# Expert rows gathered by quarters and turned on VectorE instead of TensorE, in a one-core mixture-of-experts layer

## The chip, the cores and the metric

One NeuronCore of a Trainium2 chip runs the whole layer as one program. The metric is the device time of one execution in microseconds (us). All data are float32.

## The reference

The layer takes a residual stream x of 1024 tokens by 1024 features. It runs three gated token mixers side by side (attention, a matrix memory, a gated recurrence), merges them, and adds the result to x. Then a fine-grained mixture of experts follows, which is the part that the change touches:

```python
scores = sigmoid(h @ router_w)              # 1024 tokens, 64 experts
idx, wts = top 8 experts of each token      # 8192 assignments
for each block of rows of one expert e:     # rows sorted by expert
    xb  = h[rt]                             # gather the rows of its tokens
    hid = silu(xb @ w1[e]) * (xb @ w3[e])   # 1024 -> 256
    y.at[rt].add((hid @ w2[e]) * rw)        # 256 -> 1024, scatter-add
y = y + (silu(h @ ws1) * (h @ ws3)) @ ws2   # the shared expert
```

## The kernel before

Up to about 1600 us it computes the mixers, their merge, the router (`route`, `choose`, `slots`) and the shared expert. Each token's normalised row goes to `h2_d` in DRAM, and (token, weight) pairs are scattered into per-expert lists in `list_d`, 8 lists of 128 slots for each expert, of which every partition holds one slot of every list.

Then comes the expert stage, which loops over a table of work items. An item is one expert with at most 256 tokens: a first tile of 128 rows and, if it has more, a second one. A tile with at most 64 rows runs as a half tile, on shorter matmuls. This run has 67 items with 93 tiles. For item i:

- SyncE loads the expert's weights, 2 MB for the first product (`load_up`, L483 and L484, four buffers) and 1 MB for the second (`load_down`, L488, two buffers), each as soon as an item ahead has freed its buffer.
- GpSimd gathers the item's rows from `h2_d` three items ahead (`gather`, L712, one indirect DMA for a tile, one row of 4 KB for each partition), once the list indices are there (`e_idx`) and once the rows that lay in the buffer have been turned (`e_Tb`). After that it issues the scatter-add of item i-1 (`scatter`, L716), when the scatter before has landed and VectorE has weighed the output.
- TensorE (`pe_item`) runs the first product of item i (`up`, L1285; `up_half`, L1289), then turns the rows of item i+1 so that the features lie on the partitions (`turn_rows`, L1253, eight 128x128 transposes for a tile, into PSUM), then the second product of item i-1 (`down`, L1342; `down_half`, L1348), with the transposes of the hidden rows of item i (L1387, L1391) between its two halves.
- ScalarE copies the turned rows from PSUM to `xgT` (`rows_turned`, L1732, two copies for a tile), applies silu (L1736) and copies the turned hidden rows (L1739).
- VectorE multiplies the hidden rows (L2402), takes the indices of item i+3 (L2425), weighs the output of item i-1 (L2377, L2381, L2383) and takes its lists (L2418 to L2420).

The order on each engine is that of the program; engines wait for each other through semaphores. The feature order in `h2_d` is chosen in L2205 so that partition p of a turned row block holds rows 8p to 8p+7 of the weights.

Of the kernel before, what the change touches and what calls it, by code (L numbers as in the profile page):

```python
# [15 lines left out]

# [10 lines left out]
P = 128  # L27
# [8 lines left out]
def layer_kernel(nc, a, out):  # L36
# [24 lines left out]
    with ctx:  # L61
# [140 lines left out]
        lists2 = view(4096, NE * NT, 2)  # L202
        xg = [[view(12288, D), view(13312, D)], [view(20480, D), view(9248, D)]]
        xgT = view(14336, KD, 2 * P)
# [4 lines left out]
        idx = sb("idx", [P, 4, 2], I32)  # L209
# [15 lines left out]
        NDMA = {"sh0": 2}  # L225
# [22 lines left out]
        def bank_free(u):  # L248

            if U_B + 2 <= u < U_C:  # L250
# [57 lines left out]
        s_dst, s_ls = sem("s_dst"), sem("s_ls")  # L308
# [5 lines left out]
        e_Ta, e_Tb, e_xTa, e_xTb, e_H, e_si, e_hid, e_hT, e_hc, e_O, e_ob = (  # L314
            two(n) for n in ("Ta", "Tb", "xTa", "xTb", "H", "si", "hid", "hT", "hc", "O", "ob"))
        e_w += [sem(f"e_w{b}") for b in (2, 3)]
        e_v += [sem(f"e_v{b}") for b in (2, 3)]
        e_red, e_idx, e_idx1, e_sc = (sem("e_" + n) for n in ("red", "idx", "idx1", "sc"))
        to_clear = [*e_xg[0], *e_xg[1], *e_Ta, *e_Tb, *e_xTa, *e_xTb, *e_H, *e_si, *e_hid, *e_hT, *e_hc, *e_O, *e_ob,
                    e_red, e_idx, e_idx1, e_sc, *e_w[2:], *e_v[2:]]  # L320
# [89 lines left out]
        def _(sp):  # L410
# [14 lines left out]
            def load_block(n):  # L425
# [9 lines left out]
                elif kind == "wb":  # L435
                    src = a["w_branch"][0, j].rearrange("(k p) n -> p k n", p=P)
                    dst = flat(dst).rearrange("p (k n) -> p k n", k=4)
                elif kind == "wo":
                    src = a["w_out"][0][:, BW * j:BW * (j + 1)].rearrange("(k p) n -> p k n", p=P)
                else:  # L440
                    sp.dma_start(dst[:, :, 0:FF], a["sh_w1"][0].rearrange("(p k) f -> p k f", k=KD)).then_inc(s_ring[n % 3], 16)
                    src, dst = a["sh_w3"][0].rearrange("(p k) f -> p k f", k=KD), dst[:, :, FF:2 * FF]
# [88 lines left out]
        def _(pool):  # L531
# [86 lines left out]
            for n, row in ((1, 48), (2, 40)):  # L618
                g.dma_start(mod_d[n].rearrange("(k j m) -> j k m", k=KD, j=8),
                            foxmask[row:row + 8, :].rearrange("j (k m) -> j k m", k=KD)).then_inc(s_rd, 16)  # L620
            pool.wait_ge(s_rd, 128)
# [34 lines left out]
            for n in range(48):  # L656
# [6 lines left out]
                if n == 4:  # L663
# [5 lines left out]
                    g.dma_start(rwt, a["router_w"][0].rearrange("(p k) e -> p k e", k=KD)).then_inc(s_rw, 16)  # L669
# [34 lines left out]
            pool.wait_ge(s_ls, 16 + 16 * NT * TOPK)  # L704
            rows = list_d.rearrange("(p r) c -> p r c", p=P)
# [13 lines left out]
            def fetch_first(n, q, p):  # L719
                with pool.If(n > HALF):  # L720
                    gather(xg[0][p], idx[:, q, 0:1], P).then_inc(e_xg[0][p], 16)
                with pool.Else():
                    gather(xg[0][p], idx[:, q, 0:1], HALF).then_inc(e_xg[0][p], 16)
                pool.nop()

            def fetch_second(n, q, p):
                with pool.If(n > P):
                    with pool.If(n > P + HALF):
                        gather(xg[1][p], idx[:, q, 1:2], P).then_inc(e_xg[1][p], 16)
                    with pool.Else():  # L730
                        gather(xg[1][p], idx[:, q, 1:2], HALF).then_inc(e_xg[1][p], 16)
# [15 lines left out]
            pool.wait_ge(e_Tb[0], 1)  # L747
# [6 lines left out]
            def fetch_ahead(it, q):  # L754
# [3 lines left out]
                with pool.If(n_3 > 0):  # L758
                    pool.wait_ge(e_Tb[0], now)
# [51 lines left out]
        def _(pe):  # L811
# [339 lines left out]
            def route(i):  # L1151
                pe.wait_ge(s_h2c, i + 1)
                if i == 0:
                    pe.wait_ge(s_rw, 64)
# [96 lines left out]
            def turn_rows(j, x):  # L1251
                for k in range(KD):
                    mm = t.transpose(psum[:, 2 * j + k // 4, (k % 4) * P:(k % 4 + 1) * P], x[:, k * P:(k + 1) * P], ident[:, :])  # L1253
                    if k == KD // 2 - 1:
                        mm.then_inc(e_Ta[j], 1)
                mm.then_inc(e_Tb[j], 1)

# [4 lines left out]
            for x in (*e_H, *e_hT, *e_O, e_Ta[1], e_Tb[1]):  # L1262
                pe.sem_inc(x, 1)
            turned, seconds, outs = Count(pe, "turned"), Count(pe, "seconds"), Count(pe, "outs")
            fetched = [Count(pe, f"fetched{p}", 0, 16) for p in range(2)]
# [3 lines left out]

            def turn_second(p):  # L1270
                fetched[p].up()
                outs.wait(e_ob[1])
                fetched[p].wait(e_xg[1][p])
                turn_rows(1, xg[1][p])
                turned.up()

            def turn_first(p, fetches):
                pe.wait_ge(e_xg[0][p], fetches)
                turn_rows(0, xg[0][p])
# [4 lines left out]
            def up(j, h, r, k):  # L1284
                return t.matmul(bank(4 + j), xgT[:, k, P * j:P * (j + 1)], up_piece(h, r, k), start=(k == 0), stop=(k == KD - 1))  # L1285

            def up_half(j, b, k):
                for f in range(FK):
                    mm = t.matmul(psum[HALF * f:HALF * (f + 1), 4 + j, :].rearrange("p (w n) -> p w n", w=2)[:, :, 0:P], xgT[:, k, P * j:P * j + HALF],  # L1289
                                  w13[b][:, :, k, f * P:(f + 1) * P], start=(k == 0), stop=(k == KD - 1))  # L1290
                return mm

            def up_half_first(b, now):
                for k in range(KD):
                    if k == KD // 2:
                        pe.wait_ge(e_xTb[0], now)
# [8 lines left out]
            def up_first(n, h, r, now):  # L1305

                with pe.If(n > HALF):
                    for k in range(KD):
                        if k == KD // 2:
                            pe.wait_ge(e_xTb[0], now)  # L1310
# [1186 lines left out]
```

## Time and profile before

| | before |
|---|---|
| median of 3 runs | 2582.93 us (2582.93 to 2586.4) |
| profiled execution, from its first to its last instruction | 2584.8 us |
| TensorE busy | 2512.4 us, 97% |
| VectorE, ScalarE, GpSimd busy | 1029.0, 579.2, 417.5 us |
| mean granted TensorE clock | 0.993 of full speed |
| DMA | 440.86 MB, mean 171 GB/s |

The profiled execution's own time is its span, 2584.8 us; no other time of it is given. The expert stage, as it is used below, goes from the first `up` at 1608.94 us to the last `down` at about 2562 us.

### The profile page before, as it was taken

The page shows a single profiled execution, that of the slowest core. Times are in us where ns is not written, and L with a number is a line of the kernel's source. Part 1 is how long each engine was busy: PE and PEld are TensorE (multiplying, and loading weights), DVE is VectorE, ACT ScalarE, POOL GpSimd, SP SyncE. Part 2 cuts the span into 40 slices and gives each one's busy share as a digit, 9 for nine tenths or more (in the row PEclk, how much of TensorE's full clock was granted, in tenths as well). Part 3 has the DMA queues.
Part 4 walks back from the last instruction along what each step waited for, and adds up shares of the span by engine and source line. Part 5 has one row for each costly group of instructions (what it writes and reads, how often), then busy time and mean ns, then how long its engine had stood idle before and what let it go on. Part 6 is the DMA issues. An engine that isn't in the chain of part 4 may idle for free.

```text
span 2584.8 us, 35212 instructions
## 1 busy us (share of the span) xinstructions
PE 2512.4 (97%) x9350; PEld 1271.5 (49%) x9351; DVE 1029.0 (40%) x2548; ACT 579.2 (22%) x1078; POOL 417.5 (16%) x418
## 2 busy tenths in 40 slices
PE   6999999999999999999999999999999999999996
PEld 3444555555455556555444554445444444444443
DVE  3365443444465545554245756121222122222221
ACT  3311333332311331331111121111111111211110
POOL 0000000000210000000111435122222222222221
PEclk9999999999999999999999999999999999999998
DMA  9122243432723232222333116787889889989994
GB/s 269 52 49 75 77 116 96 107 109 73 200 54 82 82 94 80 76 96 95 124 108 133 58 41 235 260 263 230 256 277 360 289 284 344 349 269 330 344 295 92
DMA packets 128164, 440.86 MB, mean 171 GB/s; under 512 B 18220, under 2 KB 20404, under 8 KB 110928
## 3 DMA queue, kind: packets, MB, share of 16 engines
q1 hardware_dynamic: 86560, 306.91, 34.3%
q0 software_dynamic: 41520, 132.86, 19.7%
q8 instruction: 50, 0.82, 0.1%
q14 instruction: 34, 0.28, 0.0%
HBM read 369.85 MB, written 77.20 MB: 173 GB/s over the span
## 4 chain that ended last, share of the span: by engine, by line
PE 93%; DMA 4%; issue 1%; DVE 0%; ACT 0%; POOLq 0%; SPq 0%; POOL 0%; DVEq 0%
PE psum L862 34%; PE psum L1285 16%; PE psum L1342 8%; PE psum L1120 6%; PE psum L1137 4%; PE psum L1289 3%; PE psum L1253 3%; PE psum L1181 2%; PE psum L1077 2%; PE psum L1348 2%; DMA out_x<-mem,put 2%; PE psum L956 2%; PE psum L946 2%; PE psum L965 1%; DMA mem<-in_exp_w 1%; PE psum L1204 1%
## 5 line engine op out<-in xcount | busy, mean ns | idle before, releaser
L862 PE MATMUL psum<-mem 128*128 128x512 f32 x2048 | 910.1, 594 | 2.0 <-ACT mem L1485 2.0
L862 PEld LDWEIGHTS psum<-mem 128*128 128x128 f32 x2048 | 377.4, 191 | 416.9 <-issue 415.9
L1285 PE MATMUL psum<-mem 128*128 x1008 | 445.2, 597 | 6.6 <-issue 5.5
L1285 PEld LDWEIGHTS psum<-mem 128*128 128x128 f32 x1008 | 191.3, 191 | 253.9 <-issue 253.7
L1342 PE MATMUL psum<-mem 128*128 128x512 f32 x504 | 234.8, 598 | 2.0 <-DMA mem<-in_exp_w 1.0
L2402 DVE TENSOR_TENSOR mem<-mem,psum 128x256 f32<-128x256 f32 x93 | 39.2, 421 | 433.4 <-ACT mem L1736 428.1
L716 POOL DMA_INDIRECT out_x<-mem,put x93 | 142.6, 1534 | 345.8 <-issue 233.2
L1532 ACT ACTIVATE mem<-psum 128x512 f32<-128x512 f32 x128 | 75.8, 595 | 494.7 <-PE psum L862 491.9
L1736 ACT ACTIVATE mem<-psum 128x256 f32<-128x256 f32 x93 | 35.7, 384 | 615.6 <-PE psum L1285 491.6
L1120 PE MATMUL psum<-mem 128*128 128x512 f32 x384 | 165.0, 592 | 0.0
L712 POOL DMA_INDIRECT mem<-h_d,idx x93 | 95.4, 1026 | 390.0 <-DVE idx L2425 144.1
L2377 DVE SCALAR_TENSOR_TENSOR mem<-psum,lst,mem 128x1024 f32<-128x1024 f32 x63 | 80.9, 1284 | 171.7 <-PE psum L1342 161.3
L1342 PEld LDWEIGHTS psum<-mem 128*128 128x128 f32 x504 | 87.8, 190 | 91.4 <-issue 91.3
L1120 PEld LDWEIGHTS psum<-mem 128*128 128x128 f32 x384 | 72.9, 190 | 91.4 <-issue 91.4
L1137 PE MATMUL psum<-mem 128*128 128x512 f32 x256 | 112.3, 593 | 0.0
L1289 PE MATMUL psum<-mem 128*64 128x256 f32 x960 | 110.2, 382 | 0.7 <-issue 0.7
L1732 ACT ACTIVATE mem<-psum 128x512 f32<-128x512 f32 x186 | 98.5, 599 | 16.9 <-PE psum L1253 14.5
L1253 PEld LDWEIGHTS psum<-ident,mem 128*128 128x128 f32 x744 | 84.4, 142 | 35.5 <-issue 34.9
L1253 PE MATMUL psum<-ident,mem 128*128 128x128 f32 x744 | 95.3, 278 | 3.8 <-DMA mem<-h_d,idx 3.0
L1289 PEld LDWEIGHTS psum<-mem 128*64 128x64 f32 x960 | 66.6, 137 | 53.8 <-issue 23.8
L1967 DVE CUSTOM_DVE_ANT_0 mem<-psum,mem 128x512 f32<-128x512 f32 (+3 forms) x96 | 52.3, 557 | 99.8 <-PE psum L946 98.1
L683 POOL DMA_INDIRECT list_d<-mem x64 | 74.4, 1163 | 61.8 <-DVE mem L2259 44.7
(378 smaller groups left out, 2370.4 us busy)
## 6 DMA issues: line engine op xcount, KB each, us to landing
mem<-in_exp_w SPq DMA_DIRECT2D x201, 1024.0 KB
mem<-in_w_in SPq DMA_DIRECT2D x16, 2048.0 KB, 13.9
proj_d<-mem SPq DMA_DIRECT2D x104, 256.0 KB, 2.0
mem<-in_ada_w POOLq DMA_DIRECT2D x16, 1024.0 KB, 6.0
mem<-proj_d POOLq DMA_DIRECT2D x56, 256.0 KB, 2.9
mem<-proj_d POOLq DMA_DIRECT2D x20, 512.0 KB, 4.8
mem<-in_ada_w SPq DMA_DIRECT2D x4, 2048.0 KB, 19.8
mem<-in_w_branch SPq DMA_DIRECT2D x3, 2048.0 KB, 8.0
```

Source lines behind the costliest of these rows:

```text
L712: return g.indirect_dma_start(x[0:n], None, h2_d, bass.IndirectOffsetOnAxis(ap=i[0:n], axis=0), bounds_check=T - 1, oob_is_err=False)
L716: return g.indirect_dma_start(y_out, bass.IndirectOffsetOnAxis(ap=i[0:n], axis=0), x[0:n], None, bounds_check=T - 1, oob_is_err=True, comp ...
L862: mm = t.matmul(bank(unit_bank(u)), l, r, start=(k == 0), stop=(k == KD - 1))
L1120: mm = t.matmul(bank(n % 3), w[:, k, j * P:(j + 1) * P], yT[br][:, k, half * BW:(half + 1) * BW], start=(k == 0), stop=(k == 3))
L1137: mm = t.matmul(bank(half + 2 * (i == 1)), hT[:, k, i * P:(i + 1) * P], slot(("wo", half))[:, k, :], start=(k == 0), stop=(k == KD - 1))
L1253: mm = t.transpose(psum[:, 2 * j + k // 4, (k % 4) * P:(k % 4 + 1) * P], x[:, k * P:(k + 1) * P], ident[:, :])
L1285: return t.matmul(bank(4 + j), xgT[:, k, P * j:P * (j + 1)], up_piece(h, r, k), start=(k == 0), stop=(k == KD - 1))
L1289: mm = t.matmul(psum[HALF * f:HALF * (f + 1), 4 + j, :].rearrange("p (w n) -> p w n", w=2)[:, :, 0:P], xgT[:, k, P * j:P * j + HALF], w13[ ...
L1342: mm = t.matmul(bank(out_bank[j] + half), hidT[p][:, k, P * j:P * (j + 1)], w2[p][:, k, half * BW:(half + 1) * BW], start=(k == 0), stop=( ...
L1532: s.activation(dst, bank(unit_bank(u)), ACT.Copy).then_inc(s_ev, 1)
L1732: s.activation(xgT[:, 4 * half:4 * half + 4, P * j:P * (j + 1)], bank(2 * j + half).rearrange("p (k n) -> p k n", n=P), ACT.Copy).then_inc ...
L2377: v.scalar_tensor_tensor(out=ob[j][p], in0=banks(out_bank[j], 2), scalar=lst[:, q, j:j + 1], in1=g2b, op0=ALU.mult, op1=ALU.mult).then_inc ...
```

## The change

The gather of a tile becomes four indirect DMAs (two for a half tile). Each brings quarter rows of 1 KB for 32 tokens: partition 32i + b gets quarter i of token b of its group. VectorE then turns the tile with one transpose instruction that works on 32x32 blocks, straight from the gather buffer into `xgT`, of which there are now two. TensorE's `turn_rows` and ScalarE's `rows_turned` go, with their semaphores. The indices have to lie on the partitions in this new order, so the lists are loaded a second time in it (`first4`, `lists4`, four DMAs each) and the index of a quarter is 4 * token + quarter. The order of features in `h2_d`, and with it the loads of `router_w`, of the shared expert's weights and of two modulation rows, follow the quarters, in more and smaller DMAs. The hidden rows' transposes move from PSUM bank 5 to bank 1. `up_second` loses its waits for the copies.

```diff
-            def gather(x, i, n):
-                return g.indirect_dma_start(x[0:n], None, h2_d, bass.IndirectOffsetOnAxis(ap=i[0:n], axis=0),
-                                            bounds_check=T - 1, oob_is_err=False)
+            h2_q = h2_d.rearrange("t (i f) -> (t i) f", i=4)
+            def gather(x, j, q, groups, s):
+                for n in range(groups):
+                    g.indirect_dma_start(x[:, 2 * P * n:2 * P * (n + 1)], None, h2_q,
+                                         bass.IndirectOffsetOnAxis(ap=idx[:, q, j, n:n + 1], axis=0),
+                                         bounds_check=4 * T - 1, oob_is_err=False).then_inc(s, 16)
...
             pool.wait_ge(s_ls, 16 + 16 * NT * TOPK)
+            by_group = list_d.rearrange("(g b r) c -> b g r c", g=4, b=32)
+            for i in range(4):
+                g.dma_start(first4[32 * i:32 * i + 32], by_group[:, :, 0:3 * NT, :]).then_inc(s_l4, 16)
...
             fetch_second(tokens(pool, 1), 1, 1)
-            pool.wait_ge(e_Tb[0], 1)
+            for i in range(4):
+                g.dma_start(lists4[32 * i:32 * i + 32], by_group).then_inc(s_l4, 16)
+            pool.wait_ge(e_T, 1)
...
-                    pool.wait_ge(e_Tb[0], now)
+                    pool.wait_ge(e_T, now)
                     pool.wait_ge(e_idx, now)
...
                 with pe.If(n > 0):
-                    pe.wait_ge(e_xTa[0], now)
+                    pe.wait_ge(e_T, before)
...
                     pe.reg_mov(n_now, tokens(pe, i + 1))
-                    with pe.If(pe.snap(n_now) > P):
-                        turn_second(1 - r)
-                    pe.nop()
-                    with pe.If(pe.snap(n_now) > 0):
-                        turn_first(1 - r, 32 * it + 16 * h + 16 + 16 * r)
-                    pe.nop()
...
-            def rows_turned(j, half):
-                s.activation(xgT[:, 4 * half:4 * half + 4, P * j:P * (j + 1)], bank(2 * j + half).rearrange("p (k n) -> p k n", n=P),
-                             ACT.Copy).then_inc((e_xTa, e_xTb)[half][j], 1)
...
+            def turn_group(j, p, groups):
+                for _ in range(groups // 2):
+                    got[j][p].up()
+                got[j][p].wait(e_xg[j][p])
+                return v.transpose(xgT[p][:, :, P * j:P * j + 32 * groups].rearrange("p k (g b) -> p g k b", g=groups),
+                                   xg[j][p][:, 0:2 * P * groups].rearrange("p (g k a) -> p g k a", g=groups, k=KD))
...
             dve.wait_ge(s_ls, 16 + 16 * NT * TOPK + 32)
+            dve.wait_ge(s_l4, 128)
...
                         n = tokens(dve, i)
+                        with dve.If(tokens(dve, i + 1) > 0):
+                            turn_rows(tokens(dve, i + 1), (q + 1) % 2)
+                        dve.nop()
                         with dve.If(n > 0):
                             hidden_rows(n, dve.snap(i + 2))
```

`turn_rows` on VectorE calls `turn_group` for the second tile, if there is one, and then for the first, with 4 groups or 2, and raises `e_T`. For item 0 it is called before `shared_out(7)` and `put_lists`. In `residual` the one L2205 instruction becomes four, one for each quarter.

## Rows read from the trace of the kernel before

**Rows 1.** Windows of the expert stage: length, busy time of engines, clock, DMA share, GB/s.

```profile
1609.00:1650.00 41.00, 37.92 (x133) 19.07 (x134) 6.77 (x22) 7.09 (x16) 7.83 (x7) 0.92 0.74 255
1650.00:1900.00 250.00, 249.28 (x884) 123.01 (x883) 52.01 (x122) 41.23 (x94) 59.19 (x46) 1.00 0.82 255
1900.00:2150.00 250.00, 249.62 (x906) 122.11 (x907) 59.41 (x149) 41.55 (x94) 62.54 (x49) 1.00 0.92 305
2150.00:2220.00 70.00, 65.63 (x291) 31.91 (x288) 18.50 (x53) 13.52 (x30) 19.61 (x16) 1.00 1.03 372
2220.00:2325.00 105.00, 103.81 (x392) 50.89 (x391) 22.03 (x56) 17.83 (x41) 24.60 (x19) 1.00 0.91 300
2325.00:2400.00 75.00, 67.98 (x337) 34.94 (x336) 21.39 (x58) 14.12 (x31) 20.30 (x16) 0.98 0.98 330
2400.00:2562.00 162.00, 158.41 (x662) 77.69 (x660) 38.50 (x93) 27.39 (x64) 38.91 (x30) 1.00 0.83 265
```

**Rows 2.** Groups by line, 1560 to 2585 us.

```profile
L716 POOL DMA_INDIRECT out_x<-mem,put x93 | 142.6, 1534 | 345.8 <-issue 233.2 <-DVE mem L2377 106.0 <-DVE mem L2383 6.7
...
L1732 ACT ACTIVATE mem<-psum 128x512 f32<-128x512 f32 x186 | 98.5, 599 | 16.9 <-PE psum L1253 14.5 <-issue 0.2
L712 POOL DMA_INDIRECT mem<-h_d,idx x93 | 95.4, 1026 | 390.0 <-DVE idx L2425 144.1 <-issue 141.0 <-PE psum L1253 103.9
L1253 PE MATMUL psum<-ident,mem 128*128 128x128 f32 x744 | 95.3, 278 | 3.8 <-DMA mem<-h_d,idx 3.0 <-issue 0.8
...
L2377 DVE SCALAR_TENSOR_TENSOR mem<-psum,lst,mem 128x1024 f32<-128x1024 f32 x63 | 80.9, 1284 | 171.7 <-PE psum L1342 161.3 <-issue 10.4
```

**Rows 3.** The chain that ended last, from 1430 us: start, length, what.

```profile
1679.42 1.75 PE psum L1253 x16
...
1903.76 6.87 PE psum L1285 x16
...
2330.77 10.93 DMA out_x<-mem,put
```

**Rows 4.** Windows for the L1253 transposes alone: busy TensorE time and their count.

```profile
1900.00:2150.00 250.00, 23.31 (x184) 20.82 (x184) 1.00 0.92 305
2150.00:2220.00 70.00, 8.36 (x64) 7.11 (x64) 1.00 1.03 372
2220.00:2325.00 105.00, 10.04 (x80) 8.93 (x80) 1.00 0.91 300
2325.00:2400.00 75.00, 9.88 (x64) 8.37 (x64) 0.98 0.98 330
```

**Rows 5.** Software DMA queue, 1120 to 1128 us, runs of 512 B: packets, MB, share.

```profile
q0 software_dynamic: 288, 1.05, 47.9%
```

**Rows 6.** The same queue, 1099 to 1106 us, runs of 2 KB.

```profile
q0 software_dynamic: 288, 1.05, 44.5%
```

**Rows 7.** GpSimd in order of time, two stretches of the expert stage.

```profile
1955.77 1.58 POOL L716 DMA_INDIRECT out_x<-mem,put  x1 [5.05 <-issue]
1958.64 1.04 POOL L712 DMA_INDIRECT mem<-h_d,idx  x1 [1.29 <-issue]
...
2379.28 1.07 POOL L712 DMA_INDIRECT mem<-h_d,idx  x1 [1.37 <-PE psum L1253]
2380.66 0.98 POOL L712 DMA_INDIRECT mem<-h_d,idx  x1 [0.31 <-issue]
```

**Rows 8.** VectorE groups before 1600 us: L2205 reads with a stride, L2206 without.

```profile
L2205 DVE SCALAR_TENSOR_TENSOR mem<-mem,stat 128x1024 f32<-128x1024 f32 x8 | 16.6, 2073 | 0.3
...
L2206 DVE TENSOR_TENSOR mem<-mem 128x1024 f32<-128x1024 f32 x8 | 9.8, 1226 | 0.3
```

**Rows 9.** In order of time, the start of the expert stage.

```profile
1597.81 0.16 DVE L2367 CAST idx<-mem 128x6 int32<-128x6 f32 x1 [4.36 <-DMA mem<-list_d]
...
1608.94 7.13 PE L1285 MATMUL psum<-mem 128*128 x16 [1.00 <-ACT mem L1732]
```

**Rows 10.** The list scatters L683: shortest, median and longest.

```profile
L683 POOL DMA_INDIRECT list_d<-mem x64: 966/973/2617, 1429.0 to 1590.3; - x64
```

More of the change, by code:

```diff
@@ L15 @@
 from contextlib import ExitStack
+from itertools import product
 import concourse.bass as bass
@@ L668, in _ @@
                     load_mod(b2b, 2, s_rw)
-                    g.dma_start(rwt, a["router_w"][0].rearrange("(p k) e -> p k e", k=KD)).then_inc(s_rw, 16)
+                    for c, z in product(range(4), range(2)):
+                        g.dma_start(rwt[32 * c:32 * c + 32, z::2, :], by_quarter(a["router_w"][0])[4 * z + c]).then_inc(s_rw, 16)
                     g.dma_start(rbias, a["router_bias"][0:1, :].partition_broadcast(P).rearrange("b o e -> b (o e)")).then_inc(s_rw, 16)
@@ L746, in _ @@
             fetch_second(tokens(pool, 1), 1, 1)
-            pool.wait_ge(e_Tb[0], 1)
+            for i in range(4):
+                g.dma_start(lists4[32 * i:32 * i + 32], by_group).then_inc(s_l4, 16)
+            pool.wait_ge(e_T, 1)
             pool.sem_inc(e_go, 1)
@@ L1261, in _ @@
             pe.wait_ge(e_clear, 1)
[L1262 removed]
+            for x in (*e_H, *e_hT, *e_O):
                 pe.sem_inc(x, 1)
[L1264 to L1265 removed]
+            seconds, outs = Count(pe, "seconds"), Count(pe, "outs")
             n_now, n_last = pe.alloc_register("n_now"), pe.alloc_register("n_last")
@@ L1314, in up_first, with up_second @@
                     with pe.If(h > 0):
-                        up_half_first(2 + r, now)
+                        up_half_first(2 + r)
                     with pe.Else():
-                        up_half_first(r, now)
+                        up_half_first(r)
                     pe.nop()
                 pe.nop()
-            def up_second(n, h, r, before):
-                turned.wait(e_xTb[1])
-                pe.wait_ge(e_hc[0], before)
-                seconds.wait(e_hc[1])
-                pe.sem_inc(e_go, 1)
+            def up_second(n, h, r):
                 seconds.up()
@@ L1431, in pe_item @@
                     pe.nop()
-                    up_first(n, h, r, now)
+                    up_first(n, h, r)
                     with pe.If(n > P):
-                        up_second(n, h, r, before)
+                        up_second(n, h, r)
                     pe.nop()
                     pe.reg_mov(n_now, tokens(pe, i + 1))
-                    with pe.If(pe.snap(n_now) > P):
-                        turn_second(1 - r)
-                    pe.nop()
-                    with pe.If(pe.snap(n_now) > 0):
-                        turn_first(1 - r, 32 * it + 16 * h + 16 + 16 * r)
-                    pe.nop()
                 pe.nop()
@@ L2424, in take_tokens @@
                 e = first_list(dve, 4 * it + q + 3)
-                v.tensor_copy(idx[:, (q + 3) % 4, :], some(lists, e, 2, 0)).then_inc(e_idx, 1)
+                v.tensor_scalar(idx[:, (q + 3) % 4, :, :], quarters(lists4[:, :, bass.ds(e, 2), 0:1]), 4.0, quad[:, :],
+                                ALU.mult, ALU.add).then_inc(e_idx, 1)
             def weigh(n, q, done, copied):
```

147 lines of the change are left out of this document (66 added, 81 removed).

## The prediction

> **What bounds the kernel now.** I read the windows of the expert stage first, since the change lives there. The reader is to see that TensorE is busy nearly all of the time (932.7 of 953 us over the seven windows), and that the DMA share differs: 0.82 and 0.83 in two long windows (412 us together), 0.92 from 1900 us, and 1.03 and 0.98 in two short windows, which are the two where TensorE falls short (65.6 of 70, 68.0 of 75) [rows 1]. So there are two kinds of stretch. In most, TensorE sets the pace; in runs of half tiles the transfers do, since such an item brings its full 3 MB of weights for half the matmuls. The highest rate, 372 GB/s, stands where TensorE waits; I take it as what the DMA engines give with this mix [rows 1]. Next come the groups by line: the transposes are 744 instructions, eight for each of 93 tiles, and GpSimd's gathers and scatters are mostly preceded by idle time [rows 2]. Their mean of 278 ns overlaps; the chain of waits prices them rightly, 1.75 us for 16, so 0.109 us each, and shows TensorE's lines end to end elsewhere [rows 3].
>
> **TensorE's transposes go.** 744 by 0.109 is 81 us [rows 2, 3]. What of it counts depends on the stretch. The 128 transposes of the two DMA-bound windows, 14 us, count nothing [rows 1, 4]. In the window from 1900 us there are 184 of them, 20.1 us; without these, 250 us at 305 GB/s become 230 us, which asks 331 GB/s on average and more in its densest parts, close to 372, so I count half, 10 us. In the window from 2220 us there are 80, 8.7 us, and 105 us at 300 GB/s would become 96 us at 328; half again, 4 us [rows 1, 4]. The remaining 744 - 128 - 184 - 80 = 352 lie where the share is 0.74 to 0.83, and count in full: 38 us [rows 1]. Sum of the gain: 52 us.
>
> **ScalarE's copies go.** 186 by 0.599 is 98.5 us busy [rows 2], beside TensorE's work: before, the turned rows of item i+1 were ready a whole second product ahead of their use. I count 0. Their waits in `up_second` go as well, at 0.
>
> **The gather in quarters, as data.** The same bytes move in runs of 1 KB instead of 4 KB. The nearest rows are loads on the same software queue: 288 packets in runs of 512 B took 47.9% of 8 us, against 44.5% of 7 us with 2 KB, so 0.213 and 0.173 us of an engine for each packet, a factor of 1.23 [rows 5, 6]. For 1 KB the factor lies between 1 and 1.23. All rows together are 8192 times 4 KB, 33.6 MB, which is 90 us at 372 GB/s, so 0 to 21 us more of the DMA engines' time. It costs only where they bind, at most a third of the stage: 0 to 7 us. I take 3.
>
> **The gather in quarters, as instructions.** 63 full tiles (the instructions of L2377 are those of full tiles) need four each and 30 half tiles two: 312 instead of 93 [rows 2]. Two in a row start 1.38 us apart, and a gather follows a scatter after 2.87 us at the earliest that I saw [rows 7]. An item with one full tile then takes GpSimd 2.87 + 4 x 1.38 = 8.4 us. TensorE needs for it 6.87 us of first product, half as much for the second, 3.44, and two transposes, together 10.5 us [rows 3]. Two full tiles: 2.87 + 8 x 1.38 and some 1.9 for the second scatter, 15.8 against 21 us (the 1.9 is the scatter's 1.53 and a gap of 0.3 [rows 2, 7]). So GpSimd fits, and the extra 219 x 1.38 = 302 us go into its idle time. This cover is not complete: the gathers stand in front of the scatter of item i-1, which waits for its weighed output from about 5 us after the gathers may start (3.44 of second product, 1.28 of weighing [rows 2]). With six or eight gathers (8 to 11 us) it goes out 3 to 6 us late, in 26 items. What is late next is the landing, which VectorE's L2432 waits for two items later. In the chain of scatters, 10.93 us from issue to landing [rows 3], four gathers still hide. From 0 to 26 x 1 us; I take 5.
>
> As a weighed rule: the Trainium skill, page "DMA: Bandwidth & Descriptors", section "Anatomy of one DMA — SWDGE (gpsimd) path", gives a software DMA about 2.0 us plus its bytes at 436 GB/s. By that figure four quarter gathers in series are 9.2 us against 3.2 for one of 512 KB, and 63 full tiles would cost up to 378 us more of latency. The rows speak against series: starts are 1.38 us apart [rows 7], so I keep the sum as it is.
>
> **VectorE's transposes come.** No row shows one. From below: a contiguous 128x1024 pass, 1.23 us; from above: the one read with a stride, 2.07 us [rows 8]. Input and output are contiguous in runs of 32, nearer to the first, so 1.2 us; 93 of them, 112 us, in an engine that is busy 20 to 27 us in 100 there [rows 1]. They stand ahead of the hidden product of the item in front. Queued behind are the hidden product, the next indices (thus GpSimd) and the weighing. For a full tile the first product (6.87 us) hides it. Behind a half tile's, about half as long, the weighing of 1.3 us, the small list copies and a turn of 1.2 to 2.4 take as long themselves, and the transposes on TensorE no longer fill the time until the hidden rows are there. A microsecond on some of 30 half tiles; 0 to 15 us, I take 3. VectorE now also waits for the gather of item i+1 before it does item i. That gather is three items ahead in order, and its deadline on TensorE is nearly what it was.
>
> **The start.** Four small `first4` loads stand before the first indices and three more gathers before item 0 (4 us), against which TensorE's transposes and the copies fall away; the first product began at 1608.94, 11 us after the indices [rows 9]. But `put_lists` comes after the turn, and VectorE then waits for all of `lists4`, 2 MB behind the gathers of item 1. I take 3 us, bounds 0 and 8. Nearer the router, four pieces of L2205 cost some 0.5 us more for each of 8 tiles [rows 8], under the shared expert's matmuls: 0. The finer loads of `router_w` and the shared weights are issued well before their use: 0.
>
> **Sum.** -52 + 3 + 5 + 3 + 3 = -38. The profiled execution took 2584.8 us, so 2547; it lies 1.9 us above the median of 2582.93, so 2545 for the median.
>
> **Rivals.** (a) TensorE's gain in full: all but the DMA-bound windows count, 608 x 0.109 = 66 us, with the costs hidden: 2517. For it: GpSimd and VectorE have room [rows 1]. Against it: 331 GB/s on average is close to 372. (b) The transfers bind more widely than the windows' means show: the 352 transposes give 38 us, the others nothing, the finer runs take 21 us and the rest of the costs 11: 2583 - 6 = 2577, with the means of 0.92 [rows 1] for it. (c) Slower, by one mechanism: GpSimd becomes the bound. Its fixed part is 67 x 2.87 + 26 x 1.9 = 241 us, so it would need the stage's 953 us at (953 - 241) / 312 = 2.28 us for one gather. One list scatter took 2.617 us, though the median is 0.973 [rows 10]; at 2.4 the stage lasts 990 us: 2620. Against it: 1.38 [rows 7].
>
> **How the numbers follow.** The forecast (2530 to 2562) has a chance of 0.53, (a) 0.15, (b) 0.20, (c) 0.12. A difference under 0.2%, 5 us, can't be told from none here. Faster is all of the forecast and (a), and 0.13 of (b): 0.81. Same is 0.05 of (b). Slower is (c) and the last 0.02 of (b): 0.14. The range goes from (a), 2515, over (b) with its costs at their upper bounds, 2590; it leaves out (c) and a little below (a).
>
> **What the profile after would show.** The L1253 and L1732 groups gone; 312 gathers near 1.0 us, starts 1.3 to 1.4 us apart; a VectorE transpose group of 1.1 to 1.3 us; the DMA share near 1 through more of the stage, and TensorE's busy share there down from 98% to about 94. The prediction is wrong if the gathers cost GpSimd more than 1.9 us each, if a turn costs above 3 us, or if TensorE waits mostly for turned rows and not for weights. More idle time could also lower its clock, which was 0.92 and 0.98 of full in two of the windows [rows 1].

## The result, and the profile after

The changed kernel takes 2571.42 us (median of 5 runs, 2569.28 to 2574.22) against 2582.93 (2579.52 to 2586.4): a ratio of 0.9955, interval 0.9943 to 0.9967, so 11.5 us faster. The forecast was 2545. The sign is right and the time lies in the range of 2515 to 2590, but 38 us were forecast, and it lies outside the 2530 to 2562 to which the forecast's own chance was given. The profiled span is 2572.2 us.

The windows of the expert stage after, which answer to [rows 1]; the columns are those of [rows 1]:

```profile
1600.00:1650.00 50.00, 25.01 (x62) 10.57 (x60) 14.90 (x36) 1.48 (x4) 23.30 (x27) 0.84 0.60 166
1650.00:1900.00 250.00, 245.62 (x724) 110.27 (x725) 84.68 (x160) 17.93 (x51) 131.06 (x117) 0.98 0.84 269
1900.00:2150.00 250.00, 244.38 (x776) 107.72 (x774) 88.91 (x178) 17.87 (x50) 123.36 (x109) 0.99 0.96 319
2150.00:2220.00 70.00, 59.05 (x217) 24.66 (x216) 26.46 (x59) 4.94 (x14) 34.74 (x32) 0.95 1.03 380
2220.00:2325.00 105.00, 101.74 (x332) 45.23 (x332) 33.72 (x70) 7.68 (x22) 52.31 (x46) 1.00 0.89 298
2325.00:2400.00 75.00, 64.57 (x272) 27.67 (x269) 28.38 (x67) 4.83 (x14) 36.22 (x33) 0.93 1.02 359
2400.00:2550.00 150.00, 142.94 (x537) 63.34 (x535) 53.60 (x110) 11.64 (x34) 66.04 (x58) 1.00 0.84 271
```

In the long stretches the stage looks as forecast: TensorE is busy in 94% or more of the time, and the DMA share is 0.96 instead of 0.92 in the one from 1900 us. In the two runs of half tiles TensorE falls short as before (59.05 of 70 us, 64.57 of 75), and the DMA engines are full in the first of them both times (1.03), but TensorE waits for other transfers there. Before, loads of expert weights are 48% of the chain of waits from 2150 to 2220 us, and no landing of a scatter is on it; after, such landings are 52% and no weight load is on it. These are the longest pieces, of the kernel before and of the changed one:

```profile
2173.60 13.75 DMA mem<-in_exp_w
2191.12 19.78 DMA mem<-in_exp_w
```

```profile
2151.05 10.44 DMA out_x<-mem,put
2162.86 10.29 DMA out_x<-mem,put
2174.50 8.09 DMA out_x<-mem,put
2183.91 7.92 DMA out_x<-mem,put
...
2205.24 6.11 DMA mem<-h_d,idx
```

In the second run, from 2325 us, landings of scatters led the chain already before (54%) and do so after (63%). What stands out in the windows is the first row: 25.01 of 50 us busy, where the kernel before had 37.92 of 41. The groups of the new instructions, by line:

```profile
L728 POOL DMA_INDIRECT mem<-h_d,idx x312 | 316.0, 1013 | 326.2 <-issue 184.0
L733 POOL DMA_INDIRECT out_x<-mem,put x93 | 144.7, 1556 | 161.0 <-issue 139.5
L2338 DVE STREAM_TRANSPOSE mem<-mem 128x1024 f32<-128x1024 f32 (+1 forms) x93 | 96.7, 1061 | 188.5 <-issue 158.0
```

**Where the gain went.** The first product of the second item began at 1620.45 us before (the first at 1608.94 [rows 9]) and begins at 1652.41 after. From there to the end of the span it is 2584.8 - 1620.45 = 964.4 us before and 2572.2 - 1652.41 = 919.8 after. The stage gained 44.6 us, and 32.0 us were lost ahead of it. Two places hold nearly all of that. The first is 900 us away from the expert stage, in the chain of waits of the changed kernel:

```profile
697.30 1.08 POOL mod_d L624 x2
698.38 3.56 POOL mod_d L627 x7
...
702.35 7.66 DMA mod_d<-foxmask
...
710.08 1.27 POOL mem L637
...
711.72 0.43 DVE mem L1978
...
712.19 0.80 PE psum L1055 x2
```

GpSimd issues the `mod_d` writes ahead of the mLSTM's first mask multiplication. Before, the same place in its timeline read

```profile
697.78 1.23 POOL L619 DMA_DIRECT2D mod_d<-foxmask  x2
700.88 1.27 POOL L629 TENSOR_TENSOR mem<-mem,upper 128x512 f32<-128x512 f32 x1 [1.87 <-DMA mod_d<-foxmask]
```

Two writes became eight, and the multiplication comes 9.2 us later, at 710.08. TensorE, which had gone on at 704.26 before, goes on at 712.19, having idled 7.2 us, and then runs its first matmuls slowly (0.80 us for two, 0.39 before). Its granted clock, 1.00 there before, was 0.50 from 712 to 720 us and 0.76 from 720 to 726: the lower of its two levels, reached during the idle time and kept for some 11 us of work, which by half the speed is 5 us more (an estimate).

```profile
712.00:720.00 8.00, 7.81 (x25) 5.22 (x26) 2.04 (x6) 0.82 (x4) 0.11 (x1) 0.50 0.28 43
720.00:726.00 6.00, 6.00 (x20) 2.84 (x19) 5.53 (x16) 1.44 (x4) 2.00 (x2) 0.76 0.29 37
```

So the later start, 7.9 us, and the clock together make everything behind 13 us late: the products of the residual stage begin at 1391.27 instead of 1378.41. The four pieces of the residual's scaling take VectorE 19.4 us in sum, 16.6 before, and item 0's first product is 13.5 us late, so they add less than 1 us.

The second place is the start of the stage, in the chain of waits and in the waits from 1600 to 1655 us (engine, line, what it waited for: sum, times, longest):

```profile
1605.50 1.70 POOL first L716 x3
1607.20 1.96 DMA first<-list_d
...
1623.78 21.11 DMA mem<-list_d
...
1652.41 2.92 PE psum L1285 x3
```

```profile
PE psum L1378 <- DVE mem L2389: 20.9, 1, 20.9
DVE lst L2383 <- DMA mem<-list_d: 19.3, 1, 19.3
POOL mem L728 <- DVE idx L2412: 19.1, 1, 19.1
...
DVE mem L2338 <- DMA mem<-h_d,idx: 4.9, 1, 4.9
```

VectorE waits 19.3 us for `lists4`, so item 0's hidden rows are late, TensorE stands for 20.9 us, and GpSimd lacks item 3's indices. Here too the clock falls in the idle time: it was 0.69 from 1625 to 1650 us and 0.84 from 1650 to 1675.

**The clock.** Over the whole execution it was 0.985 of full speed on average, 0.993 before. Behind 700 us TensorE was busy for 35.0 us while the lower level was granted, against 12.4 us before, so the lower clock costs up to 11 us more than it did, an estimate from these two numbers; what of it falls where TensorE doesn't set the pace costs nothing. The prediction named this possibility and gave it no term. No run separates it.

### The profile page after: what moved, and what is told of

It is laid out like the page before. It is cut to its first block, busy times and chain, and to the rows that moved or that the text cites. A ratio compares the mean times of both kernels' runs of the same rounds, so it can differ in the third digit from the quotient of the medians.

```text
span 2572.2 us, 34051 instructions
## 1 busy us (share of the span) xinstructions
PE 2447.4 (95%) x8606; PEld 1194.8 (46%) x8607; DVE 1132.3 (44%) x2667; ACT 480.6 (19%) x892; POOL 645.5 (25%) x658
## 4 chain that ended last, share of the span: by engine, by line
PE 86%; DMA 6%; issue 3%; DVE 2%; POOL 1%; DVEq 1%; ACT 1%; POOLq 0%; SPq 0%; ACTq 0%
PE psum L881 34%; PE psum L1285 16%; PE psum L1334 7%; PE psum L1139 6%; DMA out_x<-mem,put 4%; PE psum L1156 3%; PE psum L1096 2%; PE psum L1289 2%; PE psum L975 2%; PE psum L965 2%; PE psum L984 1%; PE psum L1340 1%; PE psum L1200 1%; DMA mem<-list_d 1%; PE psum L1223 1%
## 5 line engine op out<-in xcount | busy, mean ns | idle before, releaser
L1285 PE MATMUL psum<-mem 128*128 x1008 | 450.9, 603 | 12.8 <-issue 8.5
L728 POOL DMA_INDIRECT mem<-h_d,idx x312 | 316.0, 1013 | 326.2 <-issue 184.0
L2338 DVE STREAM_TRANSPOSE mem<-mem 128x1024 f32<-128x1024 f32 (+1 forms) x93 | 96.7, 1061 | 188.5 <-issue 158.0
L1513 ACT ACTIVATE mem<-psum 128x512 f32<-128x512 f32 x128 | 75.8, 595 | 495.2 <-PE psum L881 492.4
L574 POOL DMA_DIRECT2D mem<-in_ada_w x16 | 14.2, 890 | 420.8 <-DVE mem L1815 371.6
L692 POOL DMA_INDIRECT list_d<-mem x64 | 68.0, 1062 | 63.5 <-DVE mem L2216 46.5
L670 POOL DMA_DIRECT2D mem<-proj_d x48 | 25.8, 538 | 214.5 <-DVE mem L2128 84.0
```

What stands on the lines that cost most here:

```text
L692: g.indirect_dma_start(list_d, bass.IndirectOffsetOnAxis(ap=dest[:, i, k:k + 1], axis=0), pay[:, i, k, :], None, bounds_check=P * NE * NT ...
L728: g.indirect_dma_start(x[:, 2 * P * n:2 * P * (n + 1)], None, h2_q, bass.IndirectOffsetOnAxis(ap=idx[:, q, j, n:n + 1], axis=0), bounds_ch ...
L1285: return t.matmul(bank(4 + j), xgT[r][:, k, P * j:P * (j + 1)], up_piece(h, r, k), start=(k == 0), stop=(k == KD - 1))
L1513: s.activation(dst, bank(unit_bank(u)), ACT.Copy).then_inc(s_ev, 1)
L2338: return v.transpose(xgT[p][:, :, P * j:P * j + 32 * groups].rearrange("p k (g b) -> p g k b", g=groups), xg[j][p][:, 0:2 * P * groups].re ...
```

## The experiments

Eighteen runs were made, in six series, each on a chip of its own. One thing has to be told first, since without it the numbers can't be read: **the changed kernel has two speeds, by the series.** In two series it took 2571.7 and 2572.0 us, in a third 2610.4, while the kernel before took 2583.8 to 2586.8 in all six series. I call the chips on which it is slower slow-stepping. No chip was used in two series, so whether this belongs to the chip or to its state at that time is not shown; within a series it doesn't change. The controls:

> The changed kernel itself, unaltered, timed again beside the kernel before. The first four runs gained their 12 us ahead of the expert stage and then lost 18 to 30 us in seven steps of 3 to 8 us inside a part whose code they don't touch, some of them ended by a ScalarE instruction that waited for something the trace doesn't name. If that loss belongs to the edits (other places in the code, or other times of the transfers), this run gives 2569 to 2574 as before; if the changed kernel itself takes such steps in another execution, it gives 2590 or more.

Measured: 2571.70 (ratio 0.9950, 0.9939 to 0.9962).

> The changed kernel unaltered, on the same chip as the run below. The four edited kernels ran in one series, the control in another. In the edited ones SyncE, GpSimd, VectorE and ScalarE executed many register and branch instructions in steps of 0.7 us (210 to 228 us of such stretches behind 1590 us, 16 to 22 us in the changed kernel), and ScalarE began its activation up to 8 us after TensorE had ended the product. If this is a property of the program that the edits make, this run takes 2569 to 2575 and the one below 2587 to 2597. If it is a property of the chip or of that series, both are of one kind: 2571 here and 2538 to 2546 below, or over 2595 here.

Measured: 2610.43 (ratio 1.0100, 1.0085 to 1.0116).

> The changed kernel unaltered, as the measure for the other runs of this series. It took 2571 in two series and 2610 in a third; so either value here, and the trace should say which by the stretches of 0.7 us steps (16 to 22 us in sum, or over 200) and by ScalarE's latest start behind a product (0 or 8 us).

Measured: 2572.02 (ratio 0.9948, 0.9931 to 0.9965).

> The kernel before, unaltered, for its trace on this chip: 2580 to 2588 either way. If the chip is of the slow-stepping kind, the question is how much of it shows with 93 gathers. Theory: the steps belong to runs of software DMAs that GpSimd issues back to back; the kernel before has one to four in a run where the changed kernel has up to ten, so it shows under 60 us of such stretches and no late ScalarE start above 2 us.

Measured, beside `c2_after` and so on a chip of the first kind: 2587.74, one run, with 26 slow steps in the sense given below. It says nothing of the slow-stepping kind.

The start was edited in two places. `e1_wait` moves a wait, `e2_mod` moves writes:

```diff
-            dve.wait_ge(s_l4, 128)
...
             def take_tokens(it, q):
                 e = first_list(dve, 4 * it + q + 3)
+                dve.wait_ge(s_l4, 128)
```

> VectorE's wait for all of lists4 goes from ahead of item 0's hidden rows into take_tokens, where lists4 is first read (for item 3). Theory, the wait itself costs: the 19.3 us that VectorE waited there fall away, TensorE's 20.9 us of idle time after item 0's products with them; 2571.4 becomes 2551 to 2556. Rival, the transfers of that stretch cost (lists4's 2 MB beside weights and gathers, DMA share 0.9 to 1.0 in 1621 to 1644): the time of the landing stays, the indices of item 3 and with them its gathers are late instead, and the time falls by 5 us at most, 2566 to 2571.

```diff
-            for n, row in ((1, 48), (2, 40)):
-                for i in range(4):
-                    g.dma_start(mod_d[n, ...], foxmask[...]).then_inc(s_rd, 16)
-            pool.wait_ge(s_rd, 16 * 14)
...
             for c in range(NT):
...
+                if c == 3:
+                    for n, row in ((1, 48), (2, 40)):
+                        for i in range(4):
+                            g.dma_start(mod_d[n, ...], foxmask[...]).then_inc(s_rd, 16)
...
                 if n == 4:
+                    pool.wait_ge(s_rd, 16 * 14)
```

> The eight fine writes of mod_d, and GpSimd's wait for them, leave their place ahead of the first chunk's multiplication in the mLSTM and stand behind that of the fourth chunk; the wait stands ahead of load_mod. Theory: GpSimd's first multiplication, 9.2 us later than in the kernel before (710.08 against 700.88), starts near 699 again, TensorE does not idle at L1055, and all that follows is 12 us earlier; 2571.4 becomes 2558 to 2561. Rival, the 12.9 us by which the residual stage starts late come from somewhere else (the finer loads of the shared weights), or are taken up again by a later wait: 2568 to 2572.

`e3_both` has both edits, and `e4_late` moves the four `lists4` loads behind the gathers of item 2 as well:

> The edits of both runs above together. If the two places cost independently, the gains add: 2540 +- 4. If the start of the expert stage waits for the same transfers whichever comes first, the sum is smaller, 2550 to 2556.

> As the run above with both edits, and the four loads of lists4 are issued behind the gathers of item 2 instead of ahead of them. If the transfers of that stretch (rival of the first run) cost, the gathers of item 2 come earlier and this gains 2 to 6 us more than both edits alone; if only the wait costs, it is the same within 2 us. A loss of some us would mean that item 3's indices are now on the path.

Measured: 2603.73, 2601.26, 2593.72 and 2594.77 (ratios 1.0071, 1.0069, 1.0038, 1.0039, each within 0.0014). All lie over every expected time, and the traces show a slow-stepping chip: 323 to 343 slow steps in each, 10 in the changed kernel's first profile. The yardstick is 2610.4, from another chip of that kind: the edits gain 7, 9, 17 and 16 us. `e4_late` stays open: in the profiled executions it is 10.5 us behind `e3_both` at the seventh tile and 14 at the end, but the medians are 1 us apart, and both kernels' times spread over 10 to 15 us. GpSimd's timeline of `e2_mod` shows the first cause taken away; the multiplication no longer waits for the writes:

```profile
698.33 1.08 POOL L624 DMA_DIRECT2D mod_d<-foxmask  x2 [8.51 <-ACT foxmask L1587]
699.80 1.27 POOL L632 TENSOR_TENSOR mem<-mem,upper 128x512 f32<-128x512 f32 x1 [0.39 <-ACT mem L1591]
```

Its first product begins at 1610.5 us instead of 1620.3, but by the seventh tile the lead is down to 4 us. The wait for `lists4` swallows it: 24.7 us instead of 19.1. And in `e1_wait` the wait has only changed its place:

```profile
DVE idx L2412 <- DMA mem<-list_d: 18.9, 1, 18.9
...
POOL mem L728 <- DVE idx L2412: 21.2, 2, 19.5
```

So for `lists4` alone the rival of that run holds: the landing limits, 20 us and more behind the issue, and item 3's indices wait for it. Only with both edits is the wait for `lists4` short, 7.8 us in `e3_both` (first row):

```profile
DVE idx L2413 <- DMA mem<-list_d: 7.8, 1, 7.8
DVE lst L2383 <- DMA mem<-list_d: 6.9, 1, 6.9
```

The second row is another wait: with the edit, L2383 waits for no load but `lists` and `lists2`, and the last of them, `lists2`, landed 9 us behind its issue at 1610.23. In the changed kernel and in the one before it landed some 3.5 us behind its issue, before VectorE was ready. This wait is what is left: in `e3_both` item 0's first product begins at 1609.2 us (1608.9 before), and that of item 1 at 1627.0 (1620.5 before).

The seventh tile's first product begins at 1678.9 us in `e3_both`, 1698.9 in `c1_after`, 1700.0 in the changed kernel of the first profile and 1672.4 before. Up to there both kinds of chip run alike, so this part is sound for both: the two places cost 20 us together, and the two gains don't add (3 and 4 us each at that tile).

> The kernel with both edits (mod_d's fine writes behind the fourth chunk, the wait for lists4 in take_tokens), unaltered, once more beside the control. Program property: 2587 to 2597 again. Property of the chip of the first series: the gains of the two places show, 12 us and 15 to 20 us, so 2538 to 2546.

> The kernel with both edits of the start once more. On a chip of the slow-stepping kind it took 2594 and 2596, against 2610 for the changed kernel there: 15 us gained. On a chip of the other kind, where the changed kernel takes 2571.4 to 2572.0, the theory of the start (12 us for mod_d's writes, 15 to 20 us for the wait on lists4) gives 2538 to 2546; if the gain is given back behind the start as transfers that come later, 2553 to 2560.

> The kernel with both edits of the start, once more. On two slow-stepping chips it took 2591 to 2596 where the changed kernel takes 2610. If this chip is of the other kind (the changed kernel 2571 to 2572), the gain of 19 to 20 us that stands at the seventh tile there should last to the end: 2550 to 2554. If it is slow-stepping again, 2590 to 2597.

Measured: 2595.82, 2591.35, 2591.58, on slow-stepping chips each time. Beside 2610.4 that is 15 to 19 us gained; beside the kernel before the ratios are 1.0053, 1.0022 (1.0014 to 1.0031) and 1.0015. On a chip of the first kind both edits were never timed. 2571.7 - 19 = 2553 is an estimate from the 20 us of lead at the seventh tile, of which 15 to 19 us were left in the times of the slow-stepping chips.

**What a slow-stepping chip does.** ScalarE's timeline around one half tile in `c1_after`, and the same tile in `c2_after`:

```profile
2016.44 0.38 ACT L1716 ACTIVATE mem<-psum 128x256 f32<-128x256 f32 x1 [3.62 <-PE psum L1378]
2029.74 0.38 ACT L1713 ACTIVATE mem<-psum 128x256 f32<-128x256 f32 x1 [12.91 <-remote]
```

```profile
2003.78 0.38 ACT L1716 ACTIVATE mem<-psum 128x256 f32<-128x256 f32 x1 [3.62 <-PE psum L1378]
2009.12 0.38 ACT L1713 ACTIVATE mem<-psum 128x256 f32<-128x256 f32 x1 [4.95 <-PE psum L1289]
```

The same instruction waits 12.91 us instead of 4.95, though the product that it waits for had ended 8.0 us before it started. "remote" means that the profile found no releaser. Fifteen of the 93 tiles have such a late start, of 1.5 to 8.0 us, nearly the same ones in the slow series' kernels with this stage; no tile has one over 1 us on the first kind. GpSimd meanwhile, in `c1_after`:

```profile
2015.08 1.03 POOL L728 DMA_INDIRECT mem<-h_d,idx  x1 [4.97 <-DVE idx L2412]
...
2024.25 1.00 POOL L728 DMA_INDIRECT mem<-h_d,idx  x1 [0.30 <-issue]
2025.56 1.48 POOL L733 DMA_INDIRECT out_x<-mem,put  x1 [0.30 <-issue]
2027.34 1.58 POOL L733 DMA_INDIRECT out_x<-mem,put  x1 [0.31 <-issue]
```

Ten software DMAs in a row, and from the fourth on the register and branch instructions of SyncE, GpSimd and VectorE last 0.7 us each instead of 0.02 to 0.3. I call those that last 0.6 to 0.8 us slow steps and count them behind 1590 us: 342 in `c1_after`, 9 in `c2_after`. (The expectations speak of the time that such stretches cover instead: by my sum, with steps less than 2 us apart joined, 239 and 6 us in these two.)

**One part of the change alone.** `e10_quarters` and `e16_quarters` are the kernel before with quarter gathers and TensorE's transposes; an item's indices are four columns, 4t + i:

```diff
-                return g.indirect_dma_start(x[0:n], None, h2_d, bass.IndirectOffsetOnAxis(ap=i[0:n], axis=0),
-                                            bounds_check=T - 1, oob_is_err=False)
+                for i in range(4):
+                    g.indirect_dma_start(x[0:n, 2 * P * i:2 * P * (i + 1)], None, h2_q,
+                                         bass.IndirectOffsetOnAxis(ap=idx[0:n, q, j, i:i + 1], axis=0),
+                                         bounds_check=4 * T - 1, oob_is_err=False).then_inc(s, 16)
```

> The kernel before with one part of the change alone: each row gathered as four quarter rows, each into its place of the same partition (372 gathers of 1 KB runs, one index column each, three small VectorE operations more an item); TensorE still turns the rows. The forecast's terms for the gather as data and as instructions, 3 + 5, give 2591 (2583 to 2616). If the steps of the slow-stepping chip come from the number of gathers in a run, such a chip gives 2600 or more and the other kind 2591.

> The kernel before with its rows gathered in quarters (372 gathers) and TensorE's transposes kept, once more: 2618 on a chip of the first kind. If this chip steps slowly and the cause is the number of software DMAs in a row, the time is 2630 or more and the stretches of slow steps sum to over 150 us; if the changed kernel's other parts make them, 2618.

Measured: 2618.08 (ratio 1.0130, 1.0113 to 1.0147) on the first kind, 2691.98 (1.0399) on the slow-stepping one. On the slow-stepping chip the number of gathers alone brings the slow steps (324 of them, 273 us in sum; 10 in `e10_quarters`), with late starts of ScalarE up to 10.9 us, and it costs 33.5 us even where steps are quick. The transposes' group in `e10_quarters` shows where: 28.9 us of idle time ahead of them, 3.8 before [rows 2].

```profile
L715 POOL DMA_INDIRECT mem<-h_d,idx x372 | 369.3, 993 | 367.0 <-issue 284.4
...
L1257 PE MATMUL psum<-ident,mem 128*128 128x128 f32 x744 | 98.0, 282 | 28.9 <-DMA mem<-h_d,idx 28.9
```

It comes in steps: 4 us at the start, 9.8 at the 35th tile, 9.2 at the 56th, 7.7 at the 75th and 76th. There the chain of waits runs over the landing of a scatter, 8 to 11 us, then over the gathers issued behind it, and their landing.

**TensorE's transposes.** `e8_turn2` is the kernel before with each row transpose issued twice:

```diff
                 for k in range(KD):
-                    mm = t.transpose(...)
+                    for _ in range(2):
+                        mm = t.transpose(...)
```

> The kernel before with each of TensorE's row transposes issued twice: 744 more, 81 us of TensorE. The forecast weighted them (0.64 on average) and gives 2583 + 52 = 2635. If all but the runs of half tiles counts in full, + 66 = 2649; if the transfers bind more widely, + 38 = 2621.

Measured: 2647.28 (ratio 1.0239, 1.0222 to 1.0256), + 62.7 us, so 0.77 of each transpose's 0.109 us counts, near the expected upper value. That is the price of adding them. Where transfers are close behind TensorE, taking the same work away gives back less, so 62.7 us is an upper bound for what the change gained by it.

**The turn on VectorE.** `e9_vslow` adds `tokens(dve, 0)` three times ahead of each turn; `e15_vturn2` makes each turn twice, with a semaphore between them:

```diff
                 got[j][p].wait(e_xg[j][p])
+                dup.up()
+                v.transpose(xgT[p][...], xg[j][p][...]).then_inc(s_w2, 1)
+                dup.wait(s_w2)
                 return v.transpose(xgT[p][...], xg[j][p][...])
```

> The changed kernel with three register loads (some 0.5 us each) ahead of each of VectorE's 93 turns, so that every turn comes about 1.6 us later, more than its own length. The forecast's term for the turns is 3 us, bounds 0 and 15, since the first product hides them: + 2 to 6 us, 2574 to 2578 (2612 to 2616 on the slow-stepping kind). If the turn stands on the path at each tile, + 100 us or more; at the half tiles alone, + 48 us.

> The changed kernel with each of VectorE's 93 turns made twice, the second behind the first by a semaphore: 1.06 us and some 0.1 us more each, 108 us in sum, without register loads in between. If the first product hides the turns as the forecast had it, + 3 to 8 us. If the turn is on the path at each tile (the run with register loads lost 158 us, but on a slow-stepping chip where such loads are slow themselves), + 70 us or more; at the half tiles alone, + 20 to 35 us.

Measured: 2768.50 and 2644.49 (ratio 1.0225), both on slow-stepping chips, so + 158 and + 34.1 us against `c1_after`. The first is where its expectation has the turn on the path at each tile, the second where it has it at the half tiles alone, and the two don't agree. That such a chip stretches the added register loads explains little: 34 more of them than in `c1_after` took over 0.6 us, of 277 added ones, and VectorE's register and branch instructions took 148 us more in sum. The clock explains a part: 0.958 on average against 0.979, which is (1 - 0.958) x 2768 - (1 - 0.979) x 2609 = 61 us at most. The rest stays open. The second run added 98.7 us of turns (L2341 below; its clock was 0.975), and a third of it shows, in steps of 1 to 5 us, many of them at half tiles:

```profile
L2344 DVE STREAM_TRANSPOSE mem<-mem 128x1024 f32<-128x1024 f32 (+1 forms) x93 | 99.8, 1073 | 3.2
L2341 DVE STREAM_TRANSPOSE mem<-mem 128x1024 f32<-128x1024 f32 (+1 forms) x93 | 98.7, 1062 | 208.2 <-issue 204.4
```

**GpSimd's order and room.** `e13_split` is `e3_both` with `fetch_second` behind `add_rows` in GpSimd's loop; `e11_gap` is the changed kernel with `tokens(pool, 0)` four times ahead of each gather.

> As the run above, and GpSimd issues the gathers of an item's second tile behind the scatters of the item in front, not ahead of them, so that at most four gathers stand in front of a scatter. If gathers in front of scatters cost (the forecast's term of 5 us, bounds 0 and 26), this gains 2 to 10 us over the run above. If the gathers' own order decides, which then come 2 to 4 us later, it loses 1 to 5 us. Where sequencers step slowly, shorter runs of software DMAs should also shorten the stretches: less than 150 us of them instead of 224.

> The changed kernel with four register loads on GpSimd ahead of each of the 312 gathers, so that starts are some 2.3 us apart instead of 1.3. Rival (c) of the forecast had GpSimd become the bound from 2.28 us a gather. If that holds, GpSimd is busy end to end and the time is 2600 to 2640. If its room is larger, under 2590. If it binds already at 1.3 us, + 250 us.

Measured: 2622.99 (ratio 1.0146), 32 us slower than `e12_both` beside it, and 3089.61 (1.1956), + 479 us, both on a slow-stepping chip. The first lost, as its second expectation had it, but 32 us and not 1 to 5; why so much was not looked into. Its slow steps did shrink, from 309 to 201. The second lies over all that was expected. Starts became 2.70 us apart (2010.23 and 2012.93 in its timeline), 1.40 more, and 312 x 1.40 = 437 us. The stage, from its first product to the end of its last, grew from 968 us in `c1_after` to 1383, by 415 us, so at this spacing nearly each microsecond of GpSimd's counts. Another 55 us lie behind the last product and were not traced. Its chain of waits says the same: "POOLq L402 22%", with VectorE waiting for rows. And the slow steps are gone: 23 of them, and no start of ScalarE over 1 us late, where `e12_both`, `e13_split` and `e9_vslow` have 309, 201 and 391 on the same chip. So they hang on how close GpSimd's software DMAs follow each other, and since the steps are gone, they are not what made this run slow.

```profile
L730 POOL DMA_INDIRECT mem<-h_d,idx x312 | 315.9, 1012 | 866.3 <-issue 816.0
```

## Why the prediction was wrong

**TensorE's transposes go, -52.** Not refuted: `e8_turn2` bounds it from above, at 62.7 us. Stretch by stretch, between the same tiles' first products (us; the stretches are named by their times before, `e8_turn2` with its loss):

| stretch | transposes | my weight | gained | `e8_turn2` |
|---|---|---|---|---|
| 1651 to 1904 | 20.9 | full | 19.1 | 19.1 |
| 1904 to 2155 | 20.9 | half | 11.0 | 19.6 |
| 2155 to 2222 | 6.1 | none | -3.3 | 1.1 |
| 2222 to 2329 | 8.7 | half | 6.7 | 7.2 |
| 2329 to 2405 | 7.0 | none | -0.1 | 1.6 |
| 2405 to 2550 | 13.1 | full | 8.7 | 11.6 |

The gained column holds the costs too. Adding transposes from 1904 us costs nearly their full time, taking them away gives about half. What I had wrong is why the runs of half tiles gain nothing. I wrote that "the transfers do" set the pace there, by the weights. On the chain of waits that was so in the first run alone; in the second the landings of scatters led already before, and after the change they lead in both. With the DMA engines full there, whether the scatters are the cause or only land late because of the weights was not separated.

**The gather as data and as instructions, 3 + 5; VectorE's turns, 3.** The durations held: 312 gathers of 1.01 us, starts 1.30 us apart, turns of 1.06 us on average. The stage gained 44.6 us against a forecast of 52 - 11 = 41, so this part of the sum came out. What the terms cost apart is not known: with 62.7 us as the upper bound of the gain, they and all that was left out, the clock with it, cost at most 62.7 - 44.6 = 18 us, and 52 - 44.6 = 7 us if my weights hold. The chain of scatters, for which the 5 us stood, is 4.3% of the chain of waits in the stage before and 10.7% after. `e10_quarters` gives 33.5 us for more gathers (372) with TensorE itself waiting for them, and `e15_vturn2` 34 us for a second set of turns, more than my bound of 15 for the first. Much of both comes at half tiles, where I had looked for it. How the cost divides between gathers and turns was not separated.

**The start, 3, bounds 0 and 8.** This is the step that failed. I wrote that VectorE "waits for all of `lists4`, 2 MB behind the gathers of item 1", and gave that no time of its own. It is 19.3 us: the four loads go out with 2 MB of weights beside them (1623.11 and 1623.58 us), the last landing 21 us behind its issue. The sum had 3 us for all that is lost ahead of item 1; 32.0 were lost. None of the prediction's signs of being wrong pointed there: a gather costs GpSimd 1.01 us, a turn 1.06, and TensorE waited long for a turned row only once, 3.8 us, for item 0. `e1_wait` shows that the wait's place in the code is not the cause, `e3_both` that an earlier issue shortens it.

**The finer loads, "issued well before their use: 0".** Wrong for a reason that I didn't look for. I asked when the data are needed and not what is queued behind their issue on GpSimd. The `mod_d` writes appear nowhere in my sum, and they cost 13 us with the clock's fall behind them; `e2_mod` removed about 10 us with them, most of which then returned in the wait for `lists4`. At the seventh tile the changed kernel is 27.6 us behind the kernel before, and both edits give back 20 of them. The other 7 stand in `e3_both` as its wait of 6.9 us for `lists2`, which the kernel before doesn't have.

**Rivals.** (a)'s full gain of the transposes, 66 us, lies near the bound of 62.7, but its costs were not hidden. (b)'s time, 2577, is nearer to the measured one than my 2545, but by luck: its mechanism did not come, since the windows from 1900 and 2220 us gained 11.0 and 6.7 us, and what was lost lay ahead of the stage. (c), GpSimd as the bound from 2.28 us a gather, did not decide on the first kind of chip. But its sum was too generous: at 2.70 us it would give a stage of 241 + 312 x 2.70 = 1083 us, and in `e11_gap` it took 1383. It left out that each gather waits for indices and for a buffer. Whether the slow-stepping chips, with ratio 1.0100, lose by the same waits is not shown.

**The weighed rule.** The Trainium skill, page "DMA: Bandwidth & Descriptors", section "Anatomy of one DMA — SWDGE (gpsimd) path", made four quarter gathers 9.2 us in series. Item 0's first gather was issued at 1611.30 and its rows were turned at 1620.35, so 9.1 us, which agrees. But it is made of three steps of 1.3 and some 5 us behind the last start: the four overlap, and only the sum is that of the rule. How much of it lay beside TensorE's products behind the start of the stage was not measured.

## What to carry to other kernels

When one instruction becomes four or eight on a queue, look at what stands behind it on that engine everywhere in the kernel, not only in the stage that the change is for. Give each wait ahead of a loop a price of its own, bytes over the rate of that stretch, before it is called hidden. Read on the chain of waits what binds in each stretch before and after: a stretch can be as short of work as before and wait for something else. And time such a kernel in several series, on several chips: here the sign itself depended on it.

## What the runs showed of the hardware

On two of six chips used (and by its trace in the first measurement) GpSimd's rows of software DMAs leave the other engines alone. On four, from about the fourth DMA of a row, register and branch instructions of SyncE, GpSimd and VectorE take 0.7 us each, and ScalarE starts up to 8.0 us behind the end of the product that it waits for (10.9 in `e16_quarters`). The kernel before, with 93 gathers, shows no difference in time; with 372 it is 2618 on one kind and 2692 on the other. The shorter row of `e13_split` left 201 slow steps of 309, and starts 2.70 us apart instead of 1.30, in `e11_gap`, left 23, at a price of 479 us. A spacing between these was not tried. Why the series differ in this was not found.

In each of the two long idle times of TensorE (705 to 712 and 1630 to 1650 us of the changed kernel) its granted clock fell to 0.50 and stayed there for some 11 and 8 us of renewed work; the kernel before, without these idle times, shows 1.00 at the first place and 0.98 from 1625 to 1650.
